# Loading the weight stream two chunks at a time

## The chip, the cores and the metric

The kernel runs on one core of a Trainium2 chip. The metric is the device time of one execution in microseconds (us); the kernel before takes 1952.2 us, the median of three runs (1951.22 to 1952.47).

## The reference

One layer of a causal decoder on x of 256 tokens by 4096 channels, all in float32:

```
xn  = rmsnorm(x, norm_mix)
h   = x + token_mixing(xn, w_in, ...)          # w_in: 4096 x 5200, gate_down: 4096 x 256
      four mixers b, c, d, a (sparse, compressed, dilated, stick-breaking attention) give o_b, o_c, o_d, o_a
      merged = sum over i of sigmoid(z @ gate_up[i]) * (o_i @ w_branch_i);  h = x + merged @ w_out
q   = rmsnorm(h, norm_ffn) @ peer_wq           # product-key router: 8 heads, top 16 of 64 x 64 experts
act = gelu(rmsnorm(h, norm_ffn) @ peer_u.T)    # 4096 experts x 4096
out = h + (scatter(softmax(top scores) * act)) @ peer_v
```

The weights are some 350 MB, each is used once, and there are only 256 rows of activations. So the kernel is one long stream of weights through TensorE.

## The kernel before

**Chunks.** The weights are cut into 680 chunks. A chunk is 256 rows by up to 512 columns, laid out as 128 partitions by 1024 floats (512 KB). Chunks 0 to 175 (CH_MIX = 176) are the input projection and come from `w_in`; chunks 176 to 679 are one tensor, `stream`, of shape 504 x 128 x 1024: the mix stage (gates and branches, 176 to 263), the output projection (264 to 391), the router's projection (392 to 423), the expert keys `u` (424 to 551) and the expert values `v` (552 to 679). CH_OUT, CH_WQ, CH_U and CH_V are the first chunks of the last four.

**A chunk's way.** A ring of four places (RING = 4) holds three copies of a chunk. SyncE (SP) loads chunk s into `w_raw[:, s % 4]` (issued at L436); ScalarE (ACT) copies it to `w_hi`, rounded to the fast matmul format (`hi`, L916); VectorE (DVE) writes the rest to `w_lo` (`lo`, L1246); TensorE (PE) makes 12 matmuls of 512 columns of it (`products`, L496 to L498: hi times hi, hi times lo, lo times hi, for two row blocks and two token tiles).

**What orders it.** Every engine goes through the chunks in order, and counts in semaphores. `hi(s)` waits for the chunk's landing (`raw_loaded[s % 4]`) and until chunk s-4 has been multiplied (`chunk_used`), since it overwrites that chunk's `w_hi`. `lo(s)` waits for `hi(s)`, the matmuls of s for `lo(s)`. The load of chunk s waits until `lo(s-4)` is done (`lo_ready`), since it overwrites that chunk's `w_raw`. Between `hi(s)` and `hi(s+1)` ACT runs what `between(s)` lists (evacuations, copies, DMA issues of its own), and DVE likewise between its `lo`s; both have all side work (attention, routing, scatter) placed at fixed chunk numbers.

**GpSimd (POOL)** issues the big transfers that are not weights: x (4 MB into `rows`, L1843) once the last transposes of the mix stage are done, two 2 MB stores of h (L1851), the 4 MB reload of h (L1854) when the stage of `v` begins, and the stores of the output in pieces of 512 KB. It is a DMA queue of its own (q0 in the profile), beside SP's (q1) and ACT's (q10).

The functions that the change touches:

Of the kernel before, what the change touches and what calls it, by code (L numbers as in the profile page):

```python
# [56 lines left out]
def in_width(g):  # L57
    return 512 if g else FIRST
# [9 lines left out]
RING = 4  # L68
# [5 lines left out]
CH_MIX = NG1 * CPG  # L74
# [77 lines left out]
def raw_parts(m4):  # L152

    one, two = CPG // RING, CH_MIX // RING
    return m4 + 1 + (min(max(m4 + 1 - one, 0), two - one) if isinstance(m4, int) else two - one)
# [14 lines left out]
def build(nc, io):  # L170
# [7 lines left out]
    def at(name, shape, dt, off):  # L178
        return nc.alloc_sbuf_tensor_at(name, shape, dt, offset=off)
# [13 lines left out]
    w_raw = at("w_raw", [P, RING, 1024], F32, RG0)  # L193
# [126 lines left out]
    def sems(*names):  # L320
        return [nc.alloc_semaphore(n) for n in names]

    raw_loaded = sems(*(f"raw_loaded{i}" for i in range(RING)))
    hi_ready, lo_ready, chunk_used = sems("hi_ready", "lo_ready", "chunk_used")
# [103 lines left out]
    with nc.Block() as block:  # L428


        @block.sync
        def _(sp):
            def load(src, slot, width, used_by=None):
                if used_by is not None:
                    sp.wait_ge(lo_ready, used_by)
                sp.dma_start(w_raw[:, slot, 0:width], src).then_inc(raw_loaded[slot], 16)  # L436

            def load_xt(c):
                sp.dma_start(xt_raw[:, 2 * c:2 * c + 2, :], io["xt"][:, 2 * c:2 * c + 2, :]).then_inc(xt_loaded[c], 16)

            constants = [("ident", ident, ident_loaded), ("g_ffn", g_ffn, ident_loaded)]
            constants += [(name, t, attn_loaded) for name, t in (
                ("causal", causal), ("dil", dil), ("rope", rope), ("gains", gains),
                ("cmp_mask", cmp_mask), ("pe_t", pe_t), ("cmp_w2", cmp_w2))]

            def in_tile(chunk, cols):
                return io["w_in"][bass.ds(chunk, 1)].rearrange("a p (j n) -> (a p) j n", j=2)[:, :, cols]

            def load_in(chunk, g, slot, used_by=None):

                if used_by is not None:
                    sp.wait_ge(lo_ready, used_by)
                into = w_raw[:, slot, 0:2 * in_width(g)].rearrange("p (j n) -> p j n", j=2)
                end = FIRST + SKEW * g
                if g:
                    sp.dma_start(into[:, :, 0:512 - end], in_tile(chunk - CPG, slice(end - SKEW, W1C)))\
                        .then_inc(raw_loaded[slot], 16)
                sp.dma_start(into[:, :, in_width(g) - end:], in_tile(chunk, slice(0, end)))\
                    .then_inc(raw_loaded[slot], 16)

            for c in range(CPG):
                load_in(c, 0, c % RING, c - RING + 1 if c >= RING else None)
                if c + 1 < CPG:
                    load_xt(c + 1)
            for c in range(CPG, 3 * CPG):
                load_in(c, c // CPG, c % RING, c - RING + 1)
                if 0 <= c - CPG - CONST_AT < len(constants):
                    name, t, loaded = constants[c - CPG - CONST_AT]
                    sp.dma_start(t[:], io[name]).then_inc(loaded, 16)
            for g in range(3, NG1):  # L470
                with sp.Fori(g * CPG // RING, (g + 1) * CPG // RING) as m:
                    for c in range(RING):
                        load_in(m * RING + c, g, c, m * RING + (c - RING + 1))
            with sp.Fori(0, (CH_END - CH_MIX) // RING) as g:
                for c in range(RING):
                    load(io["stream"][bass.ds(g * RING + c, 1)].rearrange("a p n -> (a p) n"), c, 1024,
                         g * RING + (CH_MIX + c - RING + 1))
            for h in range(NT):
                sp.wait_ge(last_added, h + 1)
                sp.dma_start(io["out"][:, h, (GRP - 1) * 512:GRP * 512],  # L480
                             h_rows[:, h, (GRP - 1) * 512:GRP * 512]).then_inc(last_stored, 16)
            sp.wait_ge(last_stored, 16 * NT)
# [422 lines left out]
        def _(act):  # L905
# [4 lines left out]

            def hi(chunk, slot, width, m4):

                act.wait_ge(raw_loaded[slot], raw_parts(m4) * 16)
                if not (isinstance(chunk, int) and chunk < RING):
                    act.wait_ge(chunk_used, chunk - (RING - 1))
                nc.scalar.activation(w_hi[:, slot, 0:width], w_raw[:, slot, 0:width], ACT.Copy).then_inc(hi_ready, 1)  # L916
# [24 lines left out]
            def copy_turned(n):  # L941
                _, b, br, blocks = TURNS[n]
                act.wait_ge(turned, n + 1)
                parts, w = 64 if br == "i" else P, len(blocks) * S
                nc.scalar.activation(flat(feat[br][0:parts, blocks[0]:blocks[-1] + 1, :]), side[0:parts, b, 0:w],
                                     ACT.Copy).then_inc(turned_copied, 1)
# [279 lines left out]
            for s in range(CH_V + CPG):  # L1226
                if s < CPG:
                    act.wait_ge(xt_loaded[s], 16)
                    for k in (2 * s, 2 * s + 1):
                        nc.scalar.activation(xt_hi[:, k, :], xt_raw[:, k, :], ACT.Copy, scale=g_mix[:, k:k + 1])\  # L1230
                            .then_inc(xt_hi_done, 1)
                hi(s, s % RING, 2 * chunk_width(s), s // RING)
                between(s)

            with act.Fori(1, GRP) as m:
                for c in range(CPG):
                    hi(m * CPG + (CH_V + c), c % RING, 1024, m * (CPG // RING) + (CH_V // RING + c // RING))
# [710 lines left out]
```

## Time and profile before

| | |
|---|---|
| median of 3 runs | 1952.2 us |
| profiled execution: its own time | 1951.42 us |
| profiled execution: span | 1949.6 us |
| PE busy | 1941.9 us |
| DVE busy | 1244.2 us |
| ACT busy | 917.0 us |
| granted TensorE clock | 1.000 over the span (its level of 2.4 GHz) |
| DMA | 404.21 MB, mean 207 GB/s |

The span runs from the first to the last instruction of the profiled execution, and its own time is 1.8 us longer. "Busy" is the union of an engine's instructions. A releaser behind an idle time is the event that ended it.

### The profile page before, as it was taken

The page shows a single profiled execution, that of the slowest core. Times are in us where ns is not written, and L with a number is a line of the kernel's source. Part 1 is how long each engine was busy: PE and PEld are TensorE (multiplying, and loading weights), DVE is VectorE, ACT ScalarE, POOL GpSimd, SP SyncE. Part 2 cuts the span into 40 slices and gives each one's busy share as a digit, 9 for nine tenths or more (in the row PEclk, how much of TensorE's full clock was granted, in tenths as well). Part 3 has the DMA queues.
Part 4 walks back from the last instruction along what each step waited for, and adds up shares of the span by engine and source line. Part 5 has one row for each costly group of instructions (what it writes and reads, how often), then busy time and mean ns, then how long its engine had stood idle before and what let it go on. Part 6 is the DMA issues. An engine that isn't in the chain of part 4 may idle for free.

```text
span 1949.6 us, 26465 instructions
## 1 busy us (share of the span) xinstructions
PE 1941.9 (100%) x9252; PEld 1604.0 (82%) x9252; DVE 1244.2 (64%) x1845; ACT 917.0 (47%) x1114; POOL 28.3 (1%) x40
## 2 busy tenths in 40 slices
PE   9999999999999999999999999999999999999999
PEld 8888888888888888888888888888887788888887
DVE  6458474575556887555555555788879876444444
ACT  6544345444466655444444464444444454333332
POOL 0010000010000000000000000000000000000000
PEclk9999999999999999999999999999999999999999
DMA  9976656555655666777777676667766578666664
GB/s 331 292 190 186 214 154 173 170 162 168 190 178 173 184 193 176 257 228 215 217 224 227 216 226 222 227 217 213 215 207 196 179 248 262 206 202 204 204 204 140
DMA packets 189959, 404.21 MB, mean 207 GB/s; under 512 B 44864, under 2 KB 118976, under 8 KB 188320
## 3 DMA queue, kind: packets, MB, share of 16 engines
q1 hardware_dynamic: 167712, 360.17, 61.4%
q10 hardware_dynamic: 20256, 25.45, 3.8%
q0 software_dynamic: 1888, 17.17, 2.3%
q8 instruction: 70, 1.15, 0.2%
q14 instruction: 33, 0.27, 0.0%
HBM read 385.96 MB, written 16.78 MB: 207 GB/s over the span
## 4 chain that ended last, share of the span: by engine, by line
PE 96%; DMA 2%; DVE 1%; ACT 0%; SPq 0%; issue 0%; ACTq 0%
PE acc L496 28%; PE acc L498 28%; PE acc L497 28%; PE acc L539 3%; PE acc L541 3%; PE acc L540 3%; DMA w_raw<-in_w_in 1%; DMA w_raw<-in_stream 1%; PE side L657 1%; PE side L620 1%; DVE w_lo L1246 1%; PE side L781 1%; PE side L692 0%; PE side L590 0%; PE side L740 0%; DVE xt_lo L1787 0%
## 5 line engine op out<-in xcount | busy, mean ns | idle before, releaser
L1246 DVE TENSOR_TENSOR w_lo<-w_raw,w_hi 128x1024 fp32r<-128x1024 f32 (+1 forms) x680 | 826.0, 1216 | 654.5 <-ACT w_hi L916 651.7
L916 ACT ACTIVATE w_hi<-w_raw 128x1024 fp32r<-128x1024 f32 (+1 forms) x680 | 715.0, 1053 | 838.4 <-PE acc L498 765.1
L496 PE MATMUL acc<-w_hi,xt_hi 128*128 128x512 f32 x1660 | 652.0, 393 | 1.8 <-DVE w_lo L1246 1.8
L498 PE MATMUL acc<-w_hi,xt_lo 128*128 128x512 f32 x1660 | 646.5, 389 | 0.0
L497 PE MATMUL acc<-w_lo,xt_hi 128*128 128x512 f32 x1660 | 646.1, 389 | 0.0
L496 PEld LDWEIGHTS acc<-w_hi,xt_hi 128*128 128x128 f32 x1660 | 311.7, 188 | 68.0 <-issue 2.5
L498 PEld LDWEIGHTS acc<-w_hi,xt_lo 128*128 128x128 f32 x1660 | 311.6, 188 | 65.5
L497 PEld LDWEIGHTS acc<-w_lo,xt_hi 128*128 128x128 f32 x1660 | 311.8, 188 | 63.6 <-issue 0.2
L496 PE MATMUL acc<-w_hi,x_hi 128*128 128x512 f32 x640 | 252.3, 394 | 0.0
L498 PE MATMUL acc<-w_hi,x_lo 128*128 128x512 f32 x640 | 249.7, 390 | 0.0
L497 PE MATMUL acc<-w_lo,x_hi 128*128 128x512 f32 x640 | 249.6, 390 | 0.0
L498 PEld LDWEIGHTS acc<-w_hi,x_lo 128*128 128x128 f32 x640 | 120.1, 188 | 25.2
L497 PEld LDWEIGHTS acc<-w_lo,x_hi 128*128 128x128 f32 x640 | 120.3, 188 | 24.0
L496 PEld LDWEIGHTS acc<-w_hi,x_hi 128*128 128x128 f32 x640 | 120.2, 188 | 24.1
L1036 ACT ACTIVATE gate<-acc 128x512 f32<-128x512 f32 x64 | 34.8, 596 | 35.6 <-PE acc L498 35.6
L496 PE MATMUL acc<-w_hi,zt_hi 128*128 128x512 f32 x128 | 50.6, 395 | 0.0
L498 PE MATMUL acc<-w_hi,zt_lo 128*128 128x512 f32 x128 | 49.9, 390 | 0.0
L497 PE MATMUL acc<-w_lo,zt_hi 128*128 128x512 f32 x128 | 49.8, 389 | 0.0
L1469 DVE TENSOR_TENSOR rows<-rows,gate 128x512 f32<-128x512 f32 x48 | 31.1, 689 | 0.8
L1461 DVE TENSOR_TENSOR gate<-acc,gate 128x512 f32<-128x512 f32 x48 | 30.8, 682 | 0.0
L980 ACT ACTIVATE probs<-probs,small 128x128 f32<-128x128 f32 (+2 forms) x44 | 18.3, 418 | 25.4 <-DVE small L1374 25.3
L498 PEld LDWEIGHTS acc<-w_hi,zt_lo 128*128 128x128 f32 x128 | 24.0, 188 | 5.1
(266 smaller groups left out, 1370.5 us busy)
## 6 DMA issues: line engine op xcount, KB each, us to landing
w_raw<-in_stream SPq DMA_DIRECT2D x504, 512.0 KB, 4.2
w_raw<-in_w_in SPq DMA_DIRECT2D x16, 496.0 KB, 3.9
w_raw<-in_w_in SPq DMA_DIRECT2D x16, 480.0 KB, 3.8
w_raw<-in_w_in SPq DMA_DIRECT2D x16, 464.0 KB, 3.8
w_raw<-in_w_in SPq DMA_DIRECT2D x16, 448.0 KB, 4.0
w_raw<-in_w_in SPq DMA_DIRECT2D x16, 432.0 KB, 3.8
w_raw<-in_w_in SPq DMA_DIRECT2D x16, 416.0 KB, 3.8
w_raw<-in_w_in SPq DMA_DIRECT2D x16, 400.0 KB, 3.8
```

Of the source, the lines that this page charges most:

```text
L496: pe.matmul(o, xh, wh, start=first and j == 0, stop=False)
L497: pe.matmul(o, xh, wl, start=False, stop=False)
L498: mm = pe.matmul(o, xl, wh, start=False, stop=last and j == 1)
L539: pe.matmul(o, xh, wh, start=first and j == 0, stop=False)
L540: pe.matmul(o, xh, wl, start=False, stop=False)
L541: mm = pe.matmul(o, xl, wh, start=False, stop=last and j == 1)
L620: mm = pe.matmul(side[:, 2, w * 32:w * 32 + NCMP], cmp_w1[:, l, :], cmp_b[:, w, half * 16 + l, :], start=(half == 0 and l == 0), stop=(hal ...
L916: nc.scalar.activation(w_hi[:, slot, 0:width], w_raw[:, slot, 0:width], ACT.Copy).then_inc(hi_ready, 1)
L1036: e = nc.scalar.activation(gate[:, n % 2, h, :], acc[:, 1, h, :], ACT.Sigmoid)
L1246: nc.vector.tensor_tensor(w_lo[:, slot, 0:width], w_raw[:, slot, 0:width], w_hi[:, slot, 0:width].bitcast(F32), ALU.subtract).then_inc(lo_ ...
L1461: nc.vector.tensor_tensor(dst, acc[:, 0, h, :], gate[:, n % 2, h, :], ALU.mult)\
L1469: e = nc.vector.tensor_tensor(dst, dst, gate[:, n % 2, h, :], ALU.add)
```

## The change

From chunk 176 on SP waits once for two chunks (until the `lo` of the second of the two old chunks is done), and issues one load of 1 MB for both: chunks s and s+1, s even, into the neighbouring places c and c+1 (c = 0 or 2). In `stream` a partition's 4 KB of chunk s and of chunk s+1 lie 512 KB apart; in `w_raw` they are neighbours. The landing is counted on the semaphore of the first place of the two. The loads of chunks below 176 stay single.

```diff
 @block.sync
-            def load(src, slot, width, used_by=None):
-                if used_by is not None:
-                    sp.wait_ge(lo_ready, used_by)
-                sp.dma_start(w_raw[:, slot, 0:width], src).then_inc(raw_loaded[slot], 16)
...
             with sp.Fori(0, (CH_END - CH_MIX) // RING) as g:
-                for c in range(RING):
-                    load(io["stream"][bass.ds(g * RING + c, 1)].rearrange("a p n -> (a p) n"), c, 1024,
-                         g * RING + (CH_MIX + c - RING + 1))
+                for c in range(0, RING, 2):
+                    sp.wait_ge(lo_ready, g * RING + (CH_MIX + c - RING + 2))
+                    sp.dma_start(w_raw[:, c:c + 2, :],
+                                 io["stream"][bass.ds(g * RING + c, 2)].rearrange("a p n -> p a n"))\
+                        .then_inc(raw_loaded[c], 16)
...
             def hi(chunk, slot, width, m4):
-                act.wait_ge(raw_loaded[slot], raw_parts(m4) * 16)
+                paired = not isinstance(chunk, int) or chunk >= CH_MIX
+                act.wait_ge(raw_loaded[slot // 2 * 2 if paired else slot], raw_parts(m4) * 16)
```

## Rows read from the trace of the kernel before

**Rows 1.** Page, sections 1 and 6: busy us (share) xcount; issues with us to landing.
```profile
PE 1941.9 (100%) x9252; PEld 1604.0 (82%) x9252; DVE 1244.2 (64%) x1845; ACT 917.0 (47%) x1114; POOL 28.3 (1%) x40
...
w_raw<-in_stream SPq DMA_DIRECT2D x504, 512.0 KB, 4.2
...
rows<-in_x ACTq DMA_DIRECT2D x4, 1024.0 KB, 7.2
cmp_w<-in_cmp_w ACTq DMA_DIRECT2D x4, 1024.0 KB, 6.4
rows<-in_x POOLq DMA_DIRECT2D x1, 4096.0 KB, 15.4
...
h_rows_d<-rows POOLq DMA_DIRECT2D x2, 2048.0 KB, 10.2
...
h_rows<-h_rows_d POOLq DMA_DIRECT2D x1, 4096.0 KB, 16.6
```

**Rows 2.** Waits of the span: who waited for whom, us, times, longest.
```profile
ACT w_hi L916 <- PE acc L498: 765.1, 484, 3.5
...
ACT w_hi L916 <- DMA w_raw<-in_stream: 16.7, 5, 7.5
```

**Rows 3.** Timeline of ACT, DVE and SP, undisturbed: start, us, what [idle <-releaser].
```profile
1698.96 1.06 ACT L916 ACTIVATE w_hi<-w_raw 128x1024 fp32r<-128x1024 f32 x1 [1.66 <-PE acc L498]
...
1709.84 1.06 ACT L916 ACTIVATE w_hi<-w_raw 128x1024 fp32r<-128x1024 f32 x1 [1.66 <-PE acc L498]
...
1701.45 0.33 SPq L436 DMA_DIRECT2D w_raw<-in_stream  x1
...
1700.05 1.23 DVE L1246 TENSOR_TENSOR w_lo<-w_raw,w_hi 128x1024 fp32r<-128x1024 f32 x1 [1.49 <-ACT w_hi L916]
```

**Rows 4.** Timeline of SP and POOL at the load of x.
```profile
805.21 0.33 SPq L436 DMA_DIRECT2D w_raw<-in_stream  x1
808.42 0.33 SPq L436 DMA_DIRECT2D w_raw<-in_stream  x1
...
805.71 0.55 POOL L1843 DMA_DIRECT2D rows<-in_x  x1 [15.55 <-PE side L740]
```

**Rows 5.** Timeline of ACT and DVE at the load of x.
```profile
813.70 1.06 ACT L916 ACTIVATE w_hi<-w_raw 128x1024 fp32r<-128x1024 f32 x1 [1.66 <-PE acc L498]
821.48 1.06 ACT L916 ACTIVATE w_hi<-w_raw 128x1024 fp32r<-128x1024 f32 x1 [6.71 <-DMA w_raw<-in_stream]
822.75 1.06 ACT L916 ACTIVATE w_hi<-w_raw 128x1024 fp32r<-128x1024 f32 x1 [0.22 <-DMA w_raw<-in_stream]
...
814.79 1.23 DVE L1246 TENSOR_TENSOR w_lo<-w_raw,w_hi 128x1024 fp32r<-128x1024 f32 x1 [1.50 <-ACT w_hi L916]
```

**Rows 6.** DMA of the window 809 to 818 us: queue, packets, MB, share of 16 engines.
```profile
q0 software_dynamic: 110, 3.60, 94.7%
q1 hardware_dynamic: 65, 0.27, 7.3%
```

**Rows 7.** Timeline of SP, POOL, ACT, DVE and PE at the reload of h.
```profile
1599.85 0.33 SPq L436 DMA_DIRECT2D w_raw<-in_stream  x1
...
1597.56 0.55 POOL L1854 DMA_DIRECT2D h_rows<-h_rows_d  x1 [369.63 <-PE acc L498]
...
1605.52 1.06 ACT L916 ACTIVATE w_hi<-w_raw 128x1024 fp32r<-128x1024 f32 x1 [0.72 <-PE acc L498]
...
1614.59 1.06 ACT L916 ACTIVATE w_hi<-w_raw 128x1024 fp32r<-128x1024 f32 x1 [7.45 <-DMA w_raw<-in_stream]
...
1616.19 1.06 ACT L916 ACTIVATE w_hi<-w_raw 128x1024 fp32r<-128x1024 f32 x1
...
1618.03 1.22 DVE L1246 TENSOR_TENSOR w_lo<-w_raw,w_hi 128x1024 fp32r<-128x1024 f32 x1
...
1620.37 1.22 DVE L1246 TENSOR_TENSOR w_lo<-w_raw,w_hi 128x1024 fp32r<-128x1024 f32 x1
...
1617.06 0.47 PE L496 MATMUL acc<-w_hi,xt_hi 128*128 128x512 f32 x1 [0.75 <-DVE w_lo L1246]
```

## The prediction, made before the change was run

> **What bounds the kernel now.** I read the page first: PE is busy for 1941.9 of 1949.6 us [rows 1]. Nothing that only shortens SP's or the DMA queues' work can give back more than PE's idle time, 7.7 us over the whole span. Then the waits [rows 2]: ACT's copies into `w_hi` wait 765.1 us in 484 waits for PE (the ring is full and PE is the slow one), and only 16.7 us, in 5 waits, for a landing of the weight stream. So the weights arrive in time but in five places. Then the timeline of an undisturbed stretch [rows 3], to see how much in time. Four of ACT's copies span 1709.84 - 1698.96 = 10.88 us, so PE takes a chunk every 2.72 us. The copy at 1698.96 belongs to chunk 592 and begins when PE is through with chunk 588. DVE's `lo` of 592 ends at 1700.05 + 1.23 = 1701.28, and at 1701.45 SP issues the load into that place, of chunk 596, whose copy begins at 1709.84.
>
> From this comes a **budget**. PE starts a chunk three chunk times (8.16 us) after the moment that releases its copy, so chunk 596 at 1709.84 - 0.08 + 8.16 = 1717.92. Its copy and `lo` take 2.32 us together (from 813.70 to 814.79 + 1.23, [rows 5]). So a load that is issued at 1701.45 may land as late as 1715.6, 14.15 us after its issue, before PE stalls. The usual load takes 4.2 us [rows 1].
>
> **Where the budget is used up.** POOL's two transfers of 4 MB take 15.4 and 16.6 us [rows 1]. At the load of x, POOL issues at 805.71 and SP issues the load of chunk 276 at 805.21 and of 277 at 808.42 [rows 4]. The copies of 277 and 278 wait for their landings until 821.48 and 822.75 [rows 5]: 277 took 13.0 us, within its budget. At the reload of h, POOL issues at 1597.56, SP issues chunk 559 at 1599.85, and its copy begins at 1614.59 [rows 7]: 14.7 us, over the budget by 0.6, and PE there has its one stall of the stage, 0.75 us. In such a burst the queues take turns: of 175 packets in 9 us 110 are POOL's (0.0327 MB each) and 65 are SP's (4 KB each) [rows 6]. A burst is 4 MB in 128 such packets, and a weight chunk is 128 packets of 4 KB, so about one chunk gets through beside a burst and the rest waits behind it. After it, 512 KB more arrive every 1.3 us (821.48 to 822.75, [rows 5]).
>
> **The change, part by part.**
> SP issues 252 times less, and its waits, register steps and issues halve. SP has nothing else to do in these stages: 0 us. ACT's waits change only their semaphore: 0 us. Nothing is computed otherwise, so PE's matmuls keep their 2.72 us a chunk.
>
> The odd chunk of a pair is requested when it is today. The **even chunk is requested one chunk time later**, since the wait is now for the second of the two old chunks: its budget falls from 14.15 to 14.15 - 2.72 = 11.4 us. And the landing of both is that of 1 MB. No row shows a 1 MB load of the stream. From below: the 4.2 us of today's. From above: 7.2 us, the ACT queue's 1 MB loads of x in the crowded start; those of cmp_w, beside the stream, take 6.4 [rows 1]. I take 4.2 + 1.3 = 5.5 in quiet stretches, by the spacing of the two landings of [rows 5], and 6.4 with other traffic about.
>
> *Quiet stretches.* Chunk 596 would be requested with 597 at 1704.17 and land at 1709.7, against a copy due at 1709.84. Even at 7.2 us the copy is 1.5 us late and PE has 5.8 us in hand (11.4 - 5.5 is 5.9). Nor does lateness feed on itself: landing, two copies (2 x 1.06), the second `lo` (1.23) and the hops (0.3) are 3.6 us, with 5.5 a cycle of 9.1 us for the four chunks of the ring, against PE's 10.88. Cost 0. The two 2 MB stores take 10.2 us [rows 1]: a pair landing 1.3 us after their end, at worst 11.5 us after its issue, just meets 11.4. Cost 0, at worst 0.1 each.
>
> *Load of x.* Pair 276/277 is issued at 808.42, behind POOL's. Today 276, issued at 805.21, was ahead of it. Now both must pass: 277's landing today is the first chunk of the burst and 278's the second, so the pair lands at 822.7. `lo` of 276 ends 2.32 later, at 825.0. PE is due to start 276 at 813.70 - 0.08 + 8.16 = 821.8. **Stall 3.3 us.** From below 2.0 (the pair gets in where 277 does today, 821.45), from above 4.9 (one more chunk's place behind). Behind it, pair 278/279 lands at 825.6 against 828.1, and 280/281, issued at 826.4 after `lo` of 277, at 831.9 against 833.7: no further stall.
>
> *Reload of h.* Pair 558/559 is issued at 1599.85. Today 558 slips through before the burst. Now the pair lands where 560 does today, at 1616.17. `lo` of 558 ends at 1618.5. PE is due at 1605.52 - 0.08 + 8.16 = 1613.6. **Stall 4.9 us**, between 3.3 (landing at 1614.57) and 6.6 (1617.8). The old stall of 0.8 is inside this one and goes. An echo is possible: in this stage DVE weighs the expert matrix between its `lo`s, and takes 2.34 us a chunk (1618.03 to 1620.37, [rows 7]). So `lo` of 559 ends at 1620.8 and pair 562/563 is issued at 1621.0, where today 562 was requested as early as 1608.4. With 6.4 us it lands at 1627.4, `lo` 562 ends at 1629.7, PE is due at 1618.5 + 10.88 = 1629.4: 0.3 us, between 0 (5.5 us) and 2.4 (7.2 us, and again one turn of the ring later). Queued behind ACT's copy of 558, which now waits until 1616.2 and not 1605.5, are its issues of act_blk and its copies of the expert matrix. DVE's part for chunk 566 needs them, 8 chunks on, 21.8 us: hidden. If that cover were gone, PE would wait for each of them as DVE does.
>
> **Sum:** 3.3 + 4.9 + 0.3 - 0.8 = +7.7 us. The profiled execution would come to 1951.4 + 7.7 = 1959.1 us. The median of the runs lies 0.8 above it, so 1952.2 + 7.7 = **1959.9 us**. With the bounds: 2.0 + 3.3 + 0 - 0.8 = +4.5 to 4.9 + 6.6 + 2.4 - 0.8 = +13.1, so 1956.7 to 1965.3.
>
> One rule speaks for the change. The Trainium skill (DMA: Bandwidth & Descriptors, Bandwidth) advises batches of 1 MiB or more, for a fixed cost of about 2.0 us a transfer: 252 transfers less would be 504 us of it. But this cost could only pay where somebody waits for a landing, and the trace has 16.7 us of that in all, behind a ring that gives PE 5.8 us in hand. By the trace the gain is nil.
>
> **Rivals.**
> *Not slower: the pair gets its share early.* If the queues take turns by whole transfers and not by 4 KB rows, a pair puts twice as much through at each turn. It then lands within a burst, and if it does so by 821.8 - 2.3 = 819.5 and by 1613.6 - 2.3 = 1611.3, that is 11.1 and 11.4 us after the issue, neither burst stalls PE, and the old 0.8 us go as well: 1952.2 - 0.8 = 1951.4 us. For it: SP's packets do get served all through the burst. Against it: from 810.8 on, two and then three chunks were queued, and still 65 packets passed for 110 [rows 6], half a chunk in 9 us. The Trainium skill (DMA: Bandwidth & Descriptors, Queues, rings and completion order) says that an engine drains a whole packet of some 9 to 17 descriptors before it turns to another queue; by that rule a chunk's 8 rows per engine would pass in one turn, and so might a pair's 16. The trace disagrees: 277 took 13.0 us. Chance 0.12.
> *The ring falls behind.* If 1 MB takes over 10.88 - 3.6 = 7.3 us, the ring's cycle is longer than PE's four chunks, and PE waits once a cycle, 126 times. At 8.0 us that is 126 x 0.7 = 88 us, 2040 us. For it: the 7.2 us of the start. Against it: that was with several large loads in flight. Chance 0.06.
> *Only one burst catches it* (the issue of POOL's transfer moves by a few tenths of a us and an even chunk slips through as today): +3.3 or +4.1, 1955.5 to 1956.3. Against it: both SP issues lie 2.3 us or more behind POOL's. Chance 0.08.
>
> **The numbers.** The forecast has 0.74. No change that a measurement can tell is 3.9 us (0.2%) to either side. Faster needs half of PE's idle time of the whole span back: 0.02. Within: the first rival, a third of the last, and the low edge of the forecast: 0.19. Slower: 0.79. The range runs from 1954.5, which takes in the single burst, to 1965.5.
>
> **What the changed profile would show.** Two new idle times of PE before L496 released by DVE's `lo`, of some 3.3 us near 822 and 4.9 us near 1614; ACT's waits for the stream longer there; load issues of 1024 KB landing in 5.5 us at the median; no PE idle in the last 250 us; PE's matmul busy time as before. The prediction is wrong if PE has no new stall at the two bursts, if stalls repeat each ring cycle, or if the loads of 1 MB take more than 7.3 us.

## The result, and the profile after

The changed kernel takes 1956.55 us (median of 12 runs, 1955.07 to 1962.37) against 1951.18 us for the kernel before on the same chips (12 runs): ratio 1.003, 95% interval 1.0022 to 1.0037. It is slower by 5.4 us (4.3 to 7.2 us by the interval); the forecast was 7.7 us. A second set gave 1957.22 against 1951.06 (ratio 1.0031, 1.0021 to 1.0041). The profiled execution is a long one, 1962.37 us, with a span of 1960.5, of which 4.5 us arose before chunk 176, where the program is unchanged (the last section has more on that).

The page first: PE, then the load issues.

```profile
PE 1947.2 (99%) x9252; PEld 1607.6 (82%) x9252; DVE 1243.8 (63%) x1845; ACT 916.0 (47%) x1114; POOL 28.2 (1%) x40
...
w_raw<-in_stream SPq DMA_DIRECT2D x252, 1024.0 KB, 4.9
```

The 252 loads of 1 MB land in 4.9 us at the median, against 4.2 for 512 KB [rows 1]. The waits of the span (who waited for whom: us, times, longest):

```profile
ACT w_hi L914 <- PE acc L495: 710.3, 456, 3.5
...
ACT w_hi L914 <- DMA w_raw<-in_stream: 106.3, 45, 9.1
...
PE acc L493 <- DVE w_lo L1244: 8.0, 3, 3.5
```

ACT now waits 106.3 us for the stream in 45 waits, where it was 16.7 us in 5 [rows 2]. Nearly all of it is absorbed: PE waited for `lo` three times in the whole program, once of them at 48 us, before the change begins. The three idle times of PE behind chunk 176 that are longer than 0.1 us, the first at the load of x, the second in the first scatter round, the third at the reload of h:

```profile
828.05 0.47 PE L493 MATMUL acc<-w_hi,xt_hi 128*128 128x512 f32 x1 [1.82 <-DVE w_lo L1244]
...
1479.85 0.19 PE L778 MATMUL side<-hot_q,hot_c 128*128 128x64 bf16 x1 [0.63 <-DVE wmat L1687]
...
1625.26 0.47 PE L493 MATMUL acc<-w_hi,xt_hi 128*128 128x512 f32 x1 [2.75 <-DVE w_lo L1244]
```

In the second profile of the same kernel they are 1.52, 0.55 and 2.96 us. What led to the first and the third, on SP, POOL and ACT (the rows to compare with [rows 4, 5, 7]):

```profile
812.89 0.37 SPq L472 DMA_DIRECT2D w_raw<-in_stream  x1
...
810.18 0.54 POOL L1841 DMA_DIRECT2D rows<-in_x  x1 [15.56 <-PE side L737]
...
825.59 2.00 ACT L914 ACTIVATE w_hi<-w_raw 128x1024 fp32r<-128x1024 f32 x2 [9.08 <-DMA w_raw<-in_stream]
...
1608.79 0.37 SPq L472 DMA_DIRECT2D w_raw<-in_stream  x1
...
1606.50 0.55 POOL L1852 DMA_DIRECT2D h_rows<-h_rows_d  x1 [370.41 <-PE acc L495]
...
1622.80 1.06 ACT L914 ACTIVATE w_hi<-w_raw 128x1024 fp32r<-128x1024 f32 x1 [9.07 <-DMA w_raw<-in_stream]
```

Both pairs were requested 2.3 to 2.7 us behind POOL's transfer, as forecast, and took 12.7 us (812.89 to 825.59) and 14.0 us. I also laid the ends of all 680 chunks on PE (its increments of `chunk_used`) of the two traces side by side. Behind chunk 176 the distance grows at chunk 276 (+3.7 us), 512 (+0.8) and 558 (+3.0), and shrinks at 559 (-1.0, the old stall). Everywhere else it changes by less than 0.1 us.

Of the 3.7 us at chunk 276 only 2.0 are the stall. The windows of that place (busy time of PE, granted clock, DMA share, GB/s) show the rest:

```profile
820.00:826.00 6.00, 6.00 (x28) 1.00 0.93 387
828.70:832.10 3.40, 3.40 (x10) 0.50 0.51 155
833.00:839.00 6.00, 6.00 (x28) 1.00 0.51 201
```

Right after the idle time TensorE was granted 1.2 GHz instead of 2.4 for 3.4 us, which costs 1.7 us. In the second profile of this kernel the same came after the stall at 558 (1618.6 to 1622.0), and not at 276.

### The profile page after: what moved, and what is told of

Its sections match the earlier page's. It is cut to its first block, busy times and chain, and to the rows that moved or that the text cites. A ratio compares the mean times of both kernels' runs of the same rounds, so it can differ in the third digit from the quotient of the medians.

```text
span 1960.5 us, 25457 instructions
## 1 busy us (share of the span) xinstructions
PE 1947.2 (99%) x9252; PEld 1607.6 (82%) x9252; DVE 1243.8 (63%) x1845; ACT 916.0 (47%) x1114; POOL 28.2 (1%) x40
## 4 chain that ended last, share of the span: by engine, by line
PE 94%; DMA 3%; DVE 2%; ACT 1%; issue 0%; SPq 0%; ACTq 0%
PE acc L493 27%; PE acc L495 27%; PE acc L494 27%; PE acc L536 3%; PE acc L538 3%; PE acc L537 3%; DMA w_raw<-in_stream 2%; DMA w_raw<-in_w_in 1%; DVE w_lo L1244 1%; PE side L654 1%; PE side L617 1%; DMA xt_raw<-in_xt 1%; ACT w_hi L914 0%; PE side L778 0%; PE side L689 0%; PE side L587 0%
```

## The experiments

The ratios are to the kernel before; "stall" is PE's idle time in the profile of that kernel. Each kernel but the change has a single profile, so its stalls are those of one execution. "By the ends of the chunks" is the growth of the distance to the first trace, as above, and holds stall, restart and clock dip.

**The change again.**

> The changed kernel once more, to share the chip and the runs of the kernel before with the others. My theory (three places: the load of x, the start of the scatter rounds, the reload of h) expects 5 us over the kernel before, and PE stalls of about 2, 0.6 and 2.8 us ahead of chunk 276, in chunk 512 and ahead of chunk 558. Rival (the first profile's 9 us are mostly chance at the start and in the granted clock): the difference differs by several us between executions and the stalls do not come back.

1957.22 us against 1951.06, stalls 1.52, 0.55 and 2.96 us. They come back in the three places; the rival has only part of it right: at each stall 1.7 us depend on whether a clock dip follows.

**Is it the late request, or the shared landing?** First the late request alone: single loads, each with its own semaphore.

```diff
-                         g * RING + (CH_MIX + c - RING + 1))
+                         g * RING + (CH_MIX + c - RING + 2) if c % 2 == 0 else None)
```

> Loads of one chunk each with a semaphore each, as in the kernel before, but both of a pair are requested when the second old chunk is done: the even chunk's request is as late as in the change, the landing is not shared. If the late request alone does the harm, this costs what the change costs, about +5 us, with stalls of 2 and 2.8 us. If half of it is that the even chunk also has to wait for the odd one's bytes (one more chunk behind a burst, 1.3 us at each of the three places), the stalls shrink by 1.3 us each: about +1.5 us in all, PE stalls of 0.7 and 1.5 us. If neither matters, 0.

1955.22 us, ratio 1.0012 (1.0003 to 1.0021). The profile has these two stalls (PE), and none in chunk 512:

```profile
827.90 0.47 PE L496 MATMUL acc<-w_hi,xt_hi 128*128 128x512 f32 x1 [0.26 <-DVE w_lo L1246]
...
1621.66 0.47 PE L496 MATMUL acc<-w_hi,xt_hi 128*128 128x512 f32 x1 [1.69 <-DVE w_lo L1246]
```

Each is 1.1 to 1.6 us shorter than in the change: that is the odd chunk's 512 KB behind the burst (277 lands 1.3 us after 276 here, 559 1.1 us after 558). By the ends of the chunks everything behind chunk 176 costs +1.5 us here, with no clock dip in it, as expected. The medians say +4.2 us (interval of the ratio: +0.6 to +4.1), which doesn't settle the size: they mix executions with and without dips, and the +1.5 us is one execution's. Then the shared landing alone, every request as early as before:

```diff
-                sp.dma_start(w_raw[:, slot, 0:width], src).then_inc(raw_loaded[slot], 16)
+                sp.dma_start(w_raw[:, slot, 0:width], src).then_inc(raw_loaded[slot // 2 * 2], 16)
...
-                act.wait_ge(raw_loaded[slot], raw_parts(m4) * 16)
...
+                    act.wait_ge(raw_loaded[slot // 2 * 2], m4 * 32 + (raw_parts(last) - 2 * last) * 16)
```

> Single loads, each requested as early as in the kernel before, but both chunks of a pair count on one semaphore, and the copy of either waits for both. This is the other half of the change without the late request. My theory (each half ties the even chunk to the odd one behind a burst): 276 and 558 land before the bursts, but ACT waits for 277 and 559, which land at 821.5 and 1614.6 in the first trace; PE then stalls 2.0 us ahead of 276 and 3.3 less the old 1.0 ahead of 558; about +4 us, nearly the change's cost, and no stall in chunk 512 (513 lands 1.3 us earlier alone). Rival (the late request is what costs, late_singles' +1.5 to +2.4 is the larger part): +1 us or less here.

1956.38 us against 1950.69, ratio 1.003 (1.0019 to 1.0041). The stalls:

```profile
823.69 0.47 PE L496 MATMUL acc<-w_hi,xt_hi 128*128 128x512 f32 x1 [0.69 <-DVE w_lo L1250]
...
1617.72 0.72 PE L496 MATMUL acc<-w_hi,xt_hi 128*128 128x512 f32 x1 [1.92 <-DVE w_lo L1250]
```

None in chunk 512. By the ends of the chunks +3.75 us behind chunk 176, of which 1.7 are a clock dip after the second stall. So either half alone stalls PE at both bursts: chunk 276 and 558 were safe only because they were requested before the burst and waited for themselves alone. By the ends of the chunks the stalls are 1.0 and (3.8 - 1.7) 2.1 us, against my 2.0 and 3.3: the bursts were shorter than in the first trace (x: 11.1 against 13.0 us from its first to its last packet, h: 11.5 against 13.9).

**Undo the change in the three places only.** Chunks 272 to 291, 508 to 519 and 548 to 567 single, the other 226 pairs as they are:

```diff
+SINGLES = ((272, 292), (508, 520), (548, 568))
...
+                for s in range(first, end):
+                    sp.wait_ge(lo_ready, s - RING + 1)
+                    sp.dma_start(w_raw[:, s % RING, :], io["stream"][s - CH_MIX]).then_inc(raw_loaded[s % RING], 16)
```

> The change, but with single loads for chunks 272 to 291, 508 to 519 and 548 to 567, the three places where I see the time go. 220 of the 252 transfers stay paired, less some. My theory: the whole difference goes, within 1 us of the kernel before, with PE stalls as before (0.75 us ahead of 559 and none else after the first 50 us). Rival (pairs cost a little everywhere, through the ring or the clock): most of the 5 us stays, +4 us.

1951.03 against 1951.06 us, ratio 0.9998 (0.9989 to 1.0007). The only stall behind chunk 176 is the old one ahead of 559, 0.44 us, and no other chunk's end moves by as much as 0.1 us. So the whole loss sits in these 52 chunks, and 226 paired loads cost, and gain, nothing that the profile or the medians (-2.1 to +1.4 us) resolve.

**Make the bursts smaller.** In eight pieces under the change:

```diff
-            pool.dma_start(rows[:], io["x"]).then_inc(x_loaded, 16)
+            for n in range(GRP):
+                pool.wait_ge(chunk_used, CH_OUT + 6 + n)
+                pool.dma_start(rows[:, :, n * 512:(n + 1) * 512],
+                               io["x"][:, :, n * 512:(n + 1) * 512]).then_inc(x_loaded, 16)
```

(and the reload of h likewise, at `CH_V + 1 + 3 * n // 2`; DVE then waits for all eight pieces).

> The change with POOL's two 4 MB transfers cut in eight pieces of 512 KB each, one per chunk time (x) and two per three chunk times (h), so that no burst is ahead of the weights. My theory: the stalls at 276 and 558 go, and with them the old 0.75 us; what is left is the one in chunk 512: +0 to +1 us against the kernel before. Rival (the even chunk's late request is what hurts, whatever stands before it): +3 us or more stays, since twice the bytes are under way in those stretches for longer.

1952.93 us, ratio 1.0006 (0.9997 to 1.0016): most of the loss goes, and the stalls at 276, 558 and 559 are gone. But 0.68 us are left in chunk 512, and PE loses 0.4 and 1.2 us at chunks 564 and 566 (+1.3 us in all by the ends of the chunks, a little over the 0 to +1). There the ring does not catch up under DVE's weighing: beside POOL's pieces these pairs land 8.3 and 9.6 us after their requests. The same pieces with single loads:

> The kernel before with the same two transfers in eight pieces. The old stall ahead of 559 goes; the pairs' stalls at 564 and 566 under such pieces (0.4 and 1.2 us) should not appear, since single loads have one chunk time more in hand: -1.0 us. Rival: DVE's weighing in that stage, not the request, makes those stalls, and they appear here too: +0.5 us.

1950.74 against 1950.69 us, ratio 0.9996 (0.9988 to 1.0005). No stall behind chunk 176 in the profile, so those at 564 and 566 do come with the pairs. The ends of the chunks give -1.0 us behind 176; the medians don't resolve it. Two pieces of 2 MB, under the change and with single loads:

```diff
-            pool.dma_start(h_rows[:], io["h"]).then_inc(h_loaded, 16)
...
+            for h in range(NT):
+                pool.wait_ge(chunk_used, CH_V + 7 * h)
+                pool.dma_start(h_rows[:, h, :], io["h"][:, h, :]).then_inc(h_loaded, 16)
```

> The change with each of POOL's two 4 MB transfers cut in two of 2 MB, the second 4 (x) and 7 (h) chunks after the first. By the budget of 11.4 us a burst of 2 MB (7 us, and 1 to 2 us for the rest of a pair, some 9.5 us) no longer stalls PE: the stalls ahead of 276 and 558 go, with the old one; what is left is the one in chunk 512: 0 to +0.8 us against the kernel before. Rival (the ring does not recover between two bursts, as it did not under eight pieces in the stage of v): stalls of 1 to 2 us near 564 to 568.

> The kernel before (single loads) with the same two transfers cut in two. Only the old stall of 0.75 to 1.0 us ahead of 559 can go: -1.0 us, 1950.1 against 1951.1. If the pieces disturb more often than the one burst did: 0 to +1 us.

1953.94 us (ratio 1.0019, 1.001 to 1.0028) and 1954.26 us (1.0013, 1.0003 to 1.0024): both forecasts were wrong, though the first one's rival had the place and the size. At 276 and 558 the stalls are gone, as the budget says for a burst of 2 MB, but PE idles 1.80 and 3.88 us at chunk 564, with single loads too. The causes differ. With pairs it is the landing again (ACT's timeline):

```profile
1628.96 1.06 ACT L914 ACTIVATE w_hi<-w_raw 128x1024 fp32r<-128x1024 f32 x1 [8.60 <-DMA w_raw<-in_stream]
```

Pair 564/565 is requested at 1617.15, 1.2 us ahead of the second burst's first packet, and lands 11.8 us later. It had 10.1 us in hand, less than 11.4, because under DVE's weighing the `lo` that releases its request comes later. With single loads the timeline of DVE names another cause:

```profile
1630.78 0.69 DVE L1697 TENSOR_TENSOR wmat<-wmat,act_t 128x512 f32<-128x512 f32 x1 [9.26 <-DMA act_t<-act_blocks]
...
1631.99 1.22 DVE L1246 TENSOR_TENSOR w_lo<-w_raw,w_hi 128x1024 fp32r<-128x1024 f32 x1
```

The second burst (1618.6 to 1627.1) ran into ACT's read of `act_t`, whose packets took from 1617.1 to 1630.4; DVE waited 9.3 us for it in its part for chunk 563, and `lo` of 564 is queued behind that. (In the kernel with pairs that read was through at 1618.9, and DVE did not wait for it.) A new wait took the old one's place.

**What sets the length of the reload's burst?** Its packets took 13.9 us in the first trace and 13.6 in single_xrh, where ACT's stores of `act_blocks` (2 x 128 KB in packets of 1 KB) fall into it, and 11.4 to 11.8 us in the change, twice, late_singles and joint_landing, where ACT was held up at 558 and had not issued them. So, in the kernel before, those two stores one chunk later:

```diff
-                            take(n, (2 * i, 2 * i + 1))
+                        last = ch0 == CH_U and n == GRP - 1
+                        if not last:
+                            take(n, (2 * i, 2 * i + 1))
+                        elif i:
+                            take(n, (0, 1, 2, 3))
```

> The kernel before (single loads), with the first half of ACT's last act_blocks stores (2 x 128 KB, issued at chunk 558 inside the reload of h) moved to chunk 559, beside the other half. In the traces so far the reload's packets take 13.6 to 13.9 us where those stores fall into it (before, single_xrh) and 11.4 to 11.8 us where ACT is held up at 558 and they don't (four kernels). If the stores stretch the burst, it is 11.5 us here, 559 lands 2 us earlier and the stall ahead of 559 goes: -0.8 to -1.0 us. If the burst's length is chance or set by the single loads, it stays at 13.6 us and the stall too: 0 us.

1950.06 against 1951.14 us, ratio 0.9993 (0.9984 to 1.0002). The timeline of ACT with the stores moved, and then the DMA rows of the whole burst (queue, packets, MB, share), 14.0 us of the first trace and 12.5 us with the stores moved:

```profile
1613.17 1.06 ACT L916 ACTIVATE w_hi<-w_raw 128x1024 fp32r<-128x1024 f32 x1 [6.41 <-DMA w_raw<-in_stream]
1613.23 2.08 ACTq L1090 DMA_DIRECT2D act_blocks<-act_blk  x4
```

```profile
q0 software_dynamic: 143, 4.19, 73.4%
q1 hardware_dynamic: 314, 1.12, 20.2%
q10 hardware_dynamic: 206, 0.20, 4.0%
```

```profile
q0 software_dynamic: 143, 4.19, 80.8%
q1 hardware_dynamic: 260, 0.94, 18.7%
```

With q10 gone from the burst, its packets take 12.4 us and not the 13.9 of the first trace; I had expected 11.5. Chunk 559 lands 13.7 us after its request (14.7 before, [rows 7]), 1.0 us earlier and not 2, but inside its budget of 14.15, and PE's stall is gone: -0.9 us by the ends of the chunks. SP's queue also has fewer bytes in this burst (0.94 MB, 1.12 before), so not all of the 1.5 us need be the stores'. A closer pair is single_xrh, with the stores and nearly as many of SP's bytes (0.9 MB): 13.6 us. This version has the lowest ratio of all, though its interval still holds no change.

**Does the phase between burst and pair matter?** The change, with the reload issued two and three chunks later:

```diff
-            pool.wait_ge(chunk_used, CH_V)
+            pool.wait_ge(chunk_used, CH_V + 2)
             pool.wait_ge(h_stored, 32)
```

> The change, with the reload of h issued two chunks (5.4 us) later, so that its packets begin about 1.4 us after the request of pair 560/561 and after 558/559 has landed. By the budget (11.4 us from a pair's request to its landing) the place of the stall moves from 558 to 560 and its length follows the phase: PE idle of about 1.5 us ahead of 560, none ahead of 558, against 2.75 and 2.96 us ahead of 558 in the two profiles of the change: total +4 us over the kernel before. If the stall has to do with chunk 558 itself (its side work), it stays at 558.

> As reload_2, but three chunks later, so that the burst begins when pair 560/561 is just requested, the worst phase: PE idle of 3 to 4 us ahead of 560. Total +5.5 to +6.5 us over the kernel before. If the phase between the burst and the pairs does not matter, the stall is as in reload_2.

1959.27 us (5 runs, ratio 1.0038, 1.0025 to 1.0052) and 1962.08 us (4 runs, 1.0051, 1.0036 to 1.0066), 8.1 and 10.9 us above 1951.14: the place was forecast, the size was not. PE's idle times at the reload, two chunks later and then three:

```profile
1626.49 0.58 PE L493 MATMUL acc<-w_hi,xt_hi 128*128 128x512 f32 x1 [3.62 <-DVE w_lo L1244]
```

```profile
1628.82 0.77 PE L493 MATMUL acc<-w_hi,xt_hi 128*128 128x512 f32 x1 [6.93 <-DVE w_lo L1244]
```

Both are ahead of chunk 560, none is left at 558: the stall belongs to the pair that is requested when the burst begins, not to a chunk. I had sized it too short both times, by 2 to 4 us. Here ACT had copied 558 and its stores were out, and the bursts took 12.9 and 14.0 us, not 11.5. The phase was not what I had worked out either: the burst's packets began 1.8 us before the request of 560/561 in the first and 1.2 us after it in the second, and a request 1.2 us ahead of a burst was still caught. The pair took 14.1 and 17.4 us. And it had only 10.6 us in hand, less than 11.4, because `lo` of 557, which releases its request, is late under DVE's weighing; 14.1 - 10.6 and 17.4 - 10.6 give the two stalls. The rest of the loss is a clock dip at the reload in each, of 3.4 and 10.2 us, and the stalls at 276 and 512. The windows of the second (busy of PE, PEld, DVE, ACT, POOL, then the clock) show that a dip can begin while PE idles:

```profile
1616.00:1621.00 5.00, 5.00 (x23) 4.14 (x23) 0.00 (x0) 0.00 (x0) 0.00 (x0) 1.00 0.95 403
1624.00:1634.00 10.00, 5.18 (x12) 4.13 (x13) 6.55 (x9) 5.68 (x7) 0.00 (x0) 0.50 0.70 236
1635.00:1640.00 5.00, 5.00 (x23) 4.13 (x22) 3.71 (x7) 3.09 (x4) 0.00 (x0) 1.00 0.70 247
```

## Why the prediction held, and where it was off

**The mechanism was right.** The changed profile has the two stalls, at the two forecast chunks, released by DVE's `lo` behind a landing of the stream, and no idle time of PE in the last 250 us. single_xrh shows that nothing else in 226 pairs matters. The arithmetic of the budget carried: in the kernel before, 559 at 14.7 us overran 14.15; in the change, 12.7 and 14.0 us overran the 11.1 and 11.4 us of the two pairs, and the stalls (1.8 and 2.8) are within 0.2 us of the excess.

**"The pair lands where 278 and 560 do today" was sized too large:** 14.3 us after the request for x, measured 12.7; 16.3 for h, measured 14.0. So 3.3 us became 2.0 (idle 1.8 and the restart), and 4.9 became 3.0. For h the runs point to why. I read the landing of 560 off a burst that ACT's stores had stretched, and in the change those stores are queued behind ACT's copy of 558, the very copy that waits. I had named them there, and asked only whether somebody needs them, not what they do while they are in the way. The four bursts with these stores in them took 12.9 to 14.0 us, the five without 11.4 to 12.4; act_once, one profile, has the stores moved and nothing else. For x no such cause is there: the burst took 13.0 us in the first trace, 11.9 and 11.6 in the change, but also 11.5 in single_xrh and 11.1 in joint_landing, which request 276 as early as the kernel before. It varies by execution, and mine was a long one. The DMA rows show what goes with its length: in the two long bursts at x (13.0 and, in act_once, 13.1 us) SP's queue moved 1.1 to 1.2 MB, in the seven short ones 0.3 to 0.7 MB. Why it gets more in some executions is open.

**The echo of 0.3 us** did not come, because a load of 1 MB was sized too large. Pair 562/563 was requested 4.8 us after the landing of 558/559, as forecast, but took 5.1 us and not 6.4, and its `lo` ended at 1635.1, 1.3 us before PE was through with 561. (Quiet loads of 1 MB took 4.9 us at the median, not 5.5.) Stalls of this kind, a pair requested late under DVE's weighing, are the ones at 564 and 566 in paced_pairs: 8.3 and 9.6 us to the landing, with 8.4 and 8.8 us in hand.

**"Quiet stretches: cost 0" missed chunk 512,** +0.8 us. I checked the budget of `lo` against PE's matmuls, but in the scatter rounds PE also waits for work that stands behind `lo` on ACT and DVE. The timeline of ACT there:

```profile
1473.12 1.06 ACT L914 ACTIVATE w_hi<-w_raw 128x1024 fp32r<-128x1024 f32 x1 [4.78 <-DMA w_raw<-in_stream]
```

The pair 512/513 was requested at 1467.77, late because DVE had unpacked the picks ahead of `lo` of 509, and took 5.3 us. Behind ACT's copy stands its evacuation of the scatter's product, behind DVE's `lo` the one-hots and the add into `wmat`, and PE's next scatter waits for that add (0.63 us, the second row of PE above). In late_singles 512 lands alone, 0.9 us sooner after its request than the pair, and in joint_landing 513 takes 4.0 us, 1.3 us less than the pair; in both, as in single_xrh, the stall is absent.

**The clock** was no term of my sum. A dip costs 1.7 us and comes in some executions, so dips may be what lies between the sum by chunks (2.0 + 0.8 + 3.0 - 1.0 = 4.8 us) and the measured 5.4; the interval (4.3 to 7.2) is too wide to show it. Both profiles of the change have one dip behind chunk 176 and come to 6.4 and 6.2 us there.

**The number owes something to luck.** My stalls, echo and old stall add up to 7.7 us, and the same terms measured 2.0 + 3.0 + 0 - 1.0 = 4.0. Chunk 512 and the dips, for which I had no term, brought it back up to 5.4.

**The rivals.** The first (a pair gets its share early) fell: in the change's burst, too, chunk 276 landed only behind it (POOL's last packet at 823.3, the landing at 825.6). The Trainium skill (DMA: Bandwidth & Descriptors, Queues, rings and completion order) says that an engine typically drains a packet of some 9 to 17 descriptors before it turns. For these queues the trace disagrees: 277 alone, 8 rows for each DMA engine, took 13.0 us beside a burst, and a pair with 16 took 12.7. The ring falling behind fell: 4.9 us is far from 7.3. The small single-burst case did not occur in either profile. The Trainium skill (DMA: Bandwidth & Descriptors, Bandwidth) advises batches of 1 MiB or more. The trace agrees for the transfer itself, 4.9 us for 1 MB against 4.2 for 512 KB, but nobody was waiting for it.

## What to carry to other kernels

For a load in a ring, work out the time from its request to the latest landing that does not stall the slowest engine, and do it at the place in question, since side work shortens it (11.4 us in a quiet stretch here, 10.6 and 10.1 under DVE's weighing); compare it with the longest transfer of any other queue, not with the usual landing. Pairing loads takes one chunk time off that budget and ties the early chunk to the late one's bytes; here each of the two alone was enough to turn a hidden burst of 4 MB into a stall. And when a stall ends a wait on an in-order engine, list what that engine had queued behind it twice: who needs it, and whom it would have disturbed.

## What I had not expected of the hardware

**A clock dip after an idle time.** TensorE fell from 2.4 to 1.2 GHz for 3.4, 6.8 or 10.2 us at PE's longer idle times, while they lasted or within 0.6 us of their ends: at 1.82 us (828.7, above), 1.92 (joint_landing), 2.96 (the change again), 3.45 (at 48 us, in the change's profile), 3.59 and 4.04 (there too, in paced_pairs and late_singles), 3.62, 3.88 and 6.93 us. It did not come after 2.75 us in the change, nor after 1.80 in halves_pairs or any shorter one. So a stall of some 2 to 4 us costs about 1.6 to 2.8 us more, in some executions; a part of a dip that falls into the idle time costs nothing. The start of the program, where PE idled from 0 to 4.0 us near 45 us in different executions of unchanged code, scatters all the medians by this: the end of chunk 175 differs by up to 7.6 us between the profiles.

**The same burst takes different times.** 4 MB in 128 packets took 11.1 to 13.1 us at the load of x. All queues together moved 397 to 427 GB/s in each of the 14 bursts (x and h, nine profiles) that had no packet of ACT's in them, so a burst takes longer the more of SP's bytes pass beside it. In the four with ACT's stores, 0.14 to 0.20 MB in packets of 1 KB, it was 379 to 395 GB/s: those small packets go with a lower rate, and so with a longer burst than their bytes would make.
